# Splitting the expert weights of a fused transformer kernel tile by tile instead of two tiles at a time

## The reference, cut to what matters

```python
x = x + gt1 * (concatenate([na_x, hg_x], axis=-1) @ w_out)      # 4 groups of weights
...
q = (t @ wq)                                                    # 8 groups of weights
s = einsum('tpcd,pckd->tpck', q, sub_keys)                      # scores, then top-16 twice
...
idx, g = ..., softmax(top)
a = gelu(einsum('tpkd,td->tpk', u[idx], t))                     # 64 groups: the up stage
return einsum('tpk,tpkd->td', (g * a), v[idx])                  # the down stage
```

## Time and profile before

| | before |
|---|---|
| median of 3 runs | 2461.55 us |
| the profiled execution | 2461.23 us |
| its span, first to last instruction | 2459.4 us |
| PE busy | 2268.9 us (92%) |
| DVE busy | 1780.3 us (72%) |
| ACT busy | 924.7 us (38%) |
| POOL busy | 629.1 us (26%) |
| groups 0 to 75 on PE | 541 to 1360 us |
| mean granted TensorE clock | 0.973 |

### The profile page before, as it was taken

One profiled execution on the slowest core, in us unless ns is written; L12 is line 12 of the kernel. 1 busy time (PEld: TensorE's weight loads), 2 busy tenths in 40 slices (PEclk: granted clock), 3 DMA queues, 4 the chain that ended last, 5 costly groups with the idle time before them and its releaser, 6 DMA issues. The chain is left out here.

```text
span 2459.4 us, 32296 instructions
## 1 busy us (share of the span) xinstructions
PE 2268.9 (92%) x12787; PEld 2018.9 (82%) x12787; DVE 1780.3 (72%) x2981; ACT 924.7 (38%) x1210; POOL 629.1 (26%) x357
## 2 busy tenths in 40 slices
PE   7999887978998999899999899999999897899997
PEld 2888676756888999899999799999999575677775
DVE  6545687764589999999996687878776657654543
ACT  4222233333232333455563233333333434566332
POOL 0000232311346776532234333333330000000000
PEclk9999998989999999999999999999999999999999
DMA  6567400011236777789889999999995222012221
GB/s 249 199 238 243 148 10 1 1 65 55 87 116 225 240 237 250 249 314 349 323 323 384 354 355 349 356 361 350 348 359 178 87 86 83 29 52 69 68 87 68
DMA packets 178102, 488.72 MB, mean 199 GB/s; under 512 B 13696, under 2 KB 80384, under 8 KB 166432
## 3 DMA queue, kind: packets, MB, share of 16 engines
q1 hardware_dynamic: 141088, 352.43, 41.6%
q0 software_dynamic: 36864, 134.23, 14.2%
HBM read 432.08 MB, written 52.43 MB: 197 GB/s over the span
## 5 line engine op out<-in xcount | busy, mean ns | idle before, releaser
L1054 PE MATMUL ps<-h_high,u_high 128*128 128x384 f32 (+1 forms) x1216 | 430.2, 354 | 43.4 <-POOL u_low L1244 20.8
L1055 PE MATMUL ps<-h_low,u_high 128*128 128x384 f32 (+1 forms) x1216 | 420.7, 346 | 0.0
L1056 PE MATMUL ps<-h_high,u_low 128*128 128x384 f32 (+1 forms) x1216 | 420.7, 346 | 0.0
L1054 PE MATMUL ps<-w_high,v_high 128*128 128x384 f32 x1024 | 343.8, 336 | 12.0 <-DVE w_low L1624 12.0
L1055 PE MATMUL ps<-w_low,v_high 128*128 128x384 f32 x1024 | 343.0, 335 | 0.0
L1056 PE MATMUL ps<-w_high,v_low 128*128 128x384 f32 x1024 | 342.9, 335 | 0.0
L1054 PEld LDWEIGHTS ps<-h_high,u_high 128*128 128x128 f32 x1216 | 230.6, 190 | 58.5 <-POOL u_low L1244 23.6
L1381 ACT ACTIVATE v_high<-v_raw 128x2048 fp32r<-128x2048 f32 x64 | 122.6, 1916 | 347.0 <-PE ps L1056 347.0
L1054 PE MATMUL ps<-h_high,w_high 128*128 128x512 f32 x560 | 227.4, 406 | 24.9 <-DVE h_low L2273 10.3
L1055 PEld LDWEIGHTS ps<-h_low,u_high 128*128 128x128 f32 x1216 | 231.0, 190 | 8.3 <-issue 1.2
L1056 PEld LDWEIGHTS ps<-h_high,u_low 128*128 128x128 f32 x1216 | 230.5, 190 | 8.1
(11 more groups left out here) (424 smaller groups left out, 4464.2 us busy)
## 6 DMA issues: line engine op xcount, KB each, us to landing
v_raw<-in_peer_v SPq DMA_DIRECT2D x64, 1024.0 KB
w_raw<-in_w SPq DMA_DIRECT2D x99, 512.0 KB, 3.6
u_first<-in_uT SPq DMA_DIRECT2D x32, 1024.0 KB
u_second<-in_uT SPq DMA_DIRECT2D x32, 1024.0 KB
xT<-in_late_w SPq DMA_DIRECT2D x56, 512.0 KB, 4.3
gelu_up<-gelu SPq DMA_DIRECT2D x128, 192.0 KB
gates<-gates_sb SPq DMA_DIRECT2D x12, 2048.0 KB
weighted<-gelu_up SPq DMA_DIRECT2D x64, 384.0 KB
```

The lines of the kernel that those rows point to most:

```text
L1054: pe.matmul(out, wh, mh, start=start, stop=False)
L1055: pe.matmul(out, wh, ml, start=False, stop=False)
L1056: return pe.matmul(out, wl, mh, start=False, stop=stop)
```

## The change

The high and the low part of a group are now made by two instructions each, one for each tile, with an access pattern of 8 blocks of 128 values (`tile_of`). The semaphores `u_hi` and `u_split` count tiles instead of groups. ACT may make the high part of tile j of group g+2 when PE has finished tile j of group g, and it does so right behind the evacuation of that tile. PE waits for the low part of each tile. SP still loads whole groups, and still waits for both low parts of the group before.

```diff
+        def tile_of(group, j):
+            return group.rearrange("p (t j c) -> p t j c", j=GE, c=P)[:, :, j, :]
...
                 if g >= 2:
-                    sp.wait_ge(u_split, PIECES_BEFORE + g - 1)
+                    sp.wait_ge(u_split, PIECES_BEFORE + GE * (g - 1))
...
             for x in range(WQ_G + U_G):
                 if x + OUT_G < SPREAD_AT:
-                    pool.wait_ge(u_hi, OUT_PIECES + x + 1)
...
-                    pool.tensor_tensor(u_low[:, x % 2], u_raw[x % 2][:], u_high[:, x % 2].bitcast(F32),
-                                       ALU.subtract).then_inc(u_split, 1)
+                    for j in range(GE):
+                        pool.wait_ge(u_hi, PIECES_BEFORE + GE * (x + OUT_G) + j + 1)
+                        pool.tensor_tensor(tile_of(u_low[:, x % 2], j), tile_of(u_raw[x % 2][:], j),
+                                           tile_of(u_high[:, x % 2], j).bitcast(F32), ALU.subtract).then_inc(u_split, 1)
...
-                pe.wait_ge(u_split, OUT_PIECES + s + 1)
                 for j in range(GE):
                     x = GE * g + j
                     for m in batches_at(g, j):
                         spread(m)
+                    pe.wait_ge(u_split, PIECES_BEFORE + x + 1)
                     bank_free(x)
...
-            def high(x):
-                g = x + OUT_G
-                act.wait_ge(u_in[g % 2], 16 * (g // 2 + 1))
+            def high(g, j):
+                if j == 0:
+                    act.wait_ge(u_in[g % 2], 16 * (g // 2 + 1))
                 if g >= 2:
-                    act.wait_ge(u_mm, GE * (g - 1))
-                act.activation(u_high[:, x % 2], u_raw[x % 2][:], ACT.Copy).then_inc(u_hi, 1)
+                    act.wait_ge(u_mm, GE * (g - 2) + j + 1)
+                act.activation(tile_of(u_high[:, g % 2], j), tile_of(u_raw[g % 2][:], j), ACT.Copy).then_inc(u_hi, 1)
...
                         act.activation(gel[:, x % 4, :], ps[:, x % 4, 0:DENSE], ACT.Gelu).then_inc(u_ev, 1)
-                if g + 2 < GROUPS:
-                    high(g + 2 - OUT_G)
+                    if g + 2 < GROUPS:
+                        high(g + 2, j)
...
-            def low_u(x):
-                dve.wait_ge(u_hi, OUT_PIECES + x + 1)
-                dve.wait_ge(u_split, OUT_PIECES + x)
-                dve.tensor_tensor(u_low[:, x % 2], u_raw[x % 2][:], u_high[:, x % 2].bitcast(F32), ALU.subtract)\
-                   .then_inc(u_split, 1)
+            def low_u(g):
+                for j in range(GE):
+                    x = PIECES_BEFORE + GE * g + j
+                    dve.wait_ge(u_hi, x + 1)
+                    dve.wait_ge(u_split, x)
+                    dve.tensor_tensor(tile_of(u_low[:, g % 2], j), tile_of(u_raw[g % 2][:], j),
+                                      tile_of(u_high[:, g % 2], j).bitcast(F32), ALU.subtract).then_inc(u_split, 1)
```

More of the change, by code:

```diff
@@ L1206, in _ @@
             load(0)
-            sp.wait_ge(u_split, OUT_PIECES + WQ_G + U_G - 1)
+            sp.wait_ge(u_split, PIECES_BEFORE + GE * (GROUPS - 1))
             gate_pair(0)
@@ L1212, in _ @@
             spill(GROUPS - 2)
-            sp.wait_ge(u_split, OUT_PIECES + WQ_G + U_G)
+            sp.wait_ge(u_split, PIECES_BEFORE + GE * GROUPS)
             gate_pair(1)
@@ L1240, in _ @@
                 if x + OUT_G < SPREAD_AT:
-                    pool.wait_ge(u_hi, OUT_PIECES + x + 1)
                     if x == 0:
-                        pool.wait_ge(u_split, OUT_PIECES)
-                    pool.tensor_tensor(u_low[:, x % 2], u_raw[x % 2][:], u_high[:, x % 2].bitcast(F32),
-                                       ALU.subtract).then_inc(u_split, 1)
+                        pool.wait_ge(u_split, PIECES_BEFORE + GE * OUT_G)
+                    for j in range(GE):
+                        pool.wait_ge(u_hi, PIECES_BEFORE + GE * (x + OUT_G) + j + 1)
+                        pool.tensor_tensor(tile_of(u_low[:, x % 2], j), tile_of(u_raw[x % 2][:], j),
+                                           tile_of(u_high[:, x % 2], j).bitcast(F32), ALU.subtract).then_inc(u_split, 1)
                 for n in picks_at[x + OUT_G]:
@@ L1291, in _ @@
             for g in range(OUT_G):
-                pe.wait_ge(u_split, PIECES_BEFORE + g + 1)
                 for j in range(GE):
                     x = GE * g + j
+                    pe.wait_ge(u_split, PIECES_BEFORE + x + 1)
                     bank_free(x)
@@ L1385, in high_w @@
                 act.activation(w_high[:, g % 2], w[:, g % 2], ACT.Copy).then_inc(w_hi, 1)
-            high(-OUT_G)
+            for j in range(GE):
+                high(0, j)
             for t in range(KT):
                 act.activation(h_high[:, t, :], k.mixT[:, t, :], ACT.Copy).then_inc(h_hi, 1)
-            high(1 - OUT_G)
+            for j in range(GE):
+                high(1, j)
             for t in range(KT):
@@ L1394, in _ @@
                 if t in (1, 3, 5):
-                    high((t + 3) // 2 - OUT_G)
+                    for j in range(GE):
+                        high((t + 3) // 2, j)
             act.wait_ge(e_eps, NORMS_BEFORE + 1)
@@ L1400, in _ @@
                 act.activation(h_high[:, t, :], full[:, t, :], ACT.Identity, bias=k.mod[:, 24 + t:25 + t]).then_inc(h_hi, 1)
-            high(1)
+            for j in range(GE):
+                high(OUT_G + 1, j)
             for g in range(OUT_G, GROUPS):
@@ L1468, in low_out @@
             def low_out(g):
-                dve.wait_ge(u_hi, PIECES_BEFORE + g + 1)
-                dve.tensor_tensor(u_low[:, g % 2], u_raw[g % 2][:], u_high[:, g % 2].bitcast(F32), ALU.subtract)\
-                   .then_inc(u_split, 1)
+                for j in range(GE):
+                    dve.wait_ge(u_hi, PIECES_BEFORE + GE * g + j + 1)
+                    dve.tensor_tensor(tile_of(u_low[:, g % 2], j), tile_of(u_raw[g % 2][:], j),
+                                      tile_of(u_high[:, g % 2], j).bitcast(F32), ALU.subtract).then_inc(u_split, 1)
             low_out(0)
@@ L1627, in _ @@
                 if g >= SPREAD_AT:
-                    low_u(g - OUT_G)
+                    low_u(g)
                 for n in dots_at[g]:
```

## The result

| kernel | time, us | ratio to before |
|---|---|---|
| before | 2462.68 median (2455.9 to 2465.86, 20 runs) | |
| after | 2466.11 median (2463.04 to 2470.35, 20 runs) | 1.0015, 95% interval 1.0009 to 1.0021 |

The account below looks back on a forecast made before the run. From 705 to 1000 us DVE, held by POOL's subtracts, ends the chain that PE waits on. -11.5 -0.9 +1 = -11.4 us on 2461.2 gives 2449.8, so 2450; range 2436 to 2468 (forecast's own 2443 to 2458, chance 0.45).

Parts of the forecast that it names:

- the term that decides: DVE, 705 to 1000 us: twelve long waits on POOL fall to one half each; -11.5 us, bounds 0 and -27.
- the second rival: 705 to 1000 us: POOL's halves follow so closely that DVE waits for both; 2459 to 2461 us, chance 0.20.
- signs of being wrong: Wrong if a POOL half needs 3 us, DVE's long waits stay at 4.4 us, or PE waits for a bank.
- PE's side: 705 to 1000 us: PE's waits for POOL's `u_low`, 20.8 us before, could shrink by 15 us, to under 8.
- PE's wait for `peer_sel`: At group 43's transposes, near 1000 us: grows from 0.7 to between 2 and 10 us.
- The start: DVE's first subtract, group 0: starts about 0.85 us sooner, and PE with it, carried through; -0.9 us.
- The spread stretch: Groups 44 to 75, DVE making low parts: 0.1 us more per group to group 67; net +1 us, 0 to +3.
- The sizes: Half-size instructions: POOL 2.35 us against 4.6 whole, ACT 1.05 against 1.91, DVE 1.225 against 2.29.
- ACT's wait for loads ahead of the second `gelu`: ACT's new order puts the load wait first; priced zero, up to 5 us if a load landed 5 us later.
- The gain moves into `selected`: Same claim as the second rival: PE waits less for `u_low`, more at the transposes for `selected`; 2459 to 2461, chance 0.20.
- DVE gets slower: 705 to 1000 us: POOL starts more often amid DVE's dots and products; +12 us, 2463 to 2475 us, chance 0.13.
- DVE also sheds half: 705 to 1000 us: DVE waits 24 to 27 us less, PE regains 21.5; 2440, down to 2436 us, chance 0.22.

Follow-up runs that it names:

- the run with POOL and DVE alone: Small kernel without the computation: POOL's pair of half subtracts and one DVE instruction, here with a gather issued ahead; a cast takes up to 5.06 us.
- the two runs with the gap in some groups only: The change, POOL's second half waiting for its first in groups 17 to 43 alone (2456.96 us, 0.9970) or 4 to 16 alone (2466.13 us, 1.0010).
- the gap: The change, with POOL's second half waiting for the semaphore of its own first half; 2455.98 us, ratio 0.9966 to before.
- quarters: The change with POOL's subtract in four quarters of 512 values for a group, each waiting for the one ahead; 2463.11 us, ratio 1.0000.
- The run with 64 columns: The change with POOL subtracting only 64 of the 128 columns of each block in groups 4 to 43; 2434.47 us, ratio 0.9879.
- the run with 8 columns: The change with POOL subtracting only 8 of the 128 columns of each block in groups 4 to 43; 2428.88 us, ratio 0.9854.
- the gap with whole parts on DVE: The gap with halves in groups 4 to 43 alone, ACT and DVE instructions whole in the others; 2457.44 us, ratio 0.9974.

## Why the prediction was wrong, point by point

**The step that failed** is in the term that decides: "If no wait can be longer than one half, 2.35 us, they fall to 12 x 2.35 = 28.2 us: 16.5 us gained." Waits of 5.2 us occurred (casts of 5.4), longer than any before (4.5), since a gather's issue of 0.96 us joins POOL's pair and DVE does not get in until all three are over (the run with POOL and DVE alone). The groups 17 to 43, where gathers stand ahead of the pairs, are where it counts (the two runs with the gap in some groups only). The term was to be -11.5 us, with 0 as its upper bound; it is +4.1. Of this difference of 15.6 us the gap, which lets DVE in behind the first half, gives back 9.3 (60.4 to 51.1 us of waits); the other 6.3 us belong to the second error below. The bound was wrong too, though its condition, "if POOL's two halves run back to back without letting DVE in and act like one", came close: I had the mechanism of the second rival, and not what sets it off.

The trace of before does not show the hold: its longest casts and tensor_scalars, 4.0 us, are shorter than one subtract of 4.6 us. What it shows is a gather issued ahead of POOL's subtract, and at 801.82 and 934.35 us a cast that comes during such an issue and loses only 0.2 us. I looked at how long a POOL instruction is, and not at what stands in front of it; and it has no row with two low parts back to back, so a cap of one half was an inference, not a reading. One of the signs of being wrong that it named came in: DVE's long waits did not fall below 4.4 us.

**Under it lies a second error.** Even where the halves do let DVE in, the sum of its waits falls little: 51 us with the gap, 49 with quarters, 56 whole. The next instruction waits instead, since DVE has casts and products in a row. With half of POOL's work the sum is half. That total POOL time decides is what the prediction named and weighed lower. The two runs with fewer columns and the quarters bear it out in the main, with piece length as a correction (0.39 us of waiting for each microsecond of POOL with whole subtracts, 0.29 with pieces of 1.3 us). The prediction drew it from the Trainium skill, "Advanced Engine Details and Errata", section "GPSIMD Details", which states the conflict and gives no price. How long one wait lasts stands in the Trainium skill, "SBUF — State Buffer", section "SBUF: two separate sides": the shared pair is an exclusive lock that goes to one side for a whole instruction. The trace agrees (the cast alone with the pair ends with the first half, at 26.91 us), except behind a gather, where the measured hold spans three instructions, 5.6 us.

The prediction's own price of these waits, some 48 us, left out the eight dots into `row_sum` (4.4 us) and a gate product at 723 us (4.1 us); with them it is the 56.3 us of the table.

**PE's side** was to fall under 8 us of waits and is at 20.1. This goes with DVE: POOL waited 64.2 us for dots instead of 50.3. The early half is there; it is of little use as long as POOL starts late.

**PE's wait for `peer_sel`** was to grow to between 2 and 10 us and is 1.5; `selected` was to come near 987 us and starts at 1000.5. Both belong to the failed term.

**The start**, -0.9 us: measured -0.8. **The spread stretch**, +1 us, from 0 to +3: measured +0.5. Its cost side holds as worked out: from group 44 to group 66 DVE's period is 11.91 us instead of 11.81 (262.0 and 259.8 us for 22 groups). **The sizes** on POOL, ACT and DVE hold within 3%. **ACT's wait for loads ahead of the second `gelu`** does not appear under that name. ACT's idle time ahead of `gelu` that the profile puts down to the stores of `gelu` grew from 139 to 191 us; which part of it is the load that now stands ahead is not shown. PE waited for no bank, so the price of zero holds.

**The rivals.** "The gain moves into `selected`" gave 2459 to 2461 us. Of its two halves one is right, PE and POOL gain nothing; but the waiting did not move to the transposes (L1327 now, 1.5 us), it stayed at `u_low`. "DVE gets slower" gave 2463 to 2475, and the time fell in there, by another mechanism: not the dots, whose waits fell from 17.5 to 14.4 us, but the casts, from 9.1 to 26.5. "DVE also sheds half" was priced at 21.5 us of returned waits. The run with 64 columns, in which DVE's waits are halved, is some 30 us faster than before (POOL also delivers sooner in it), since the clock comes back as well. Against the run with 8 columns a wait of PE in this stretch costs 1.3 to 1.5 times its length (27.6 us for the 21.5 of before, 31.7 for the 21.6 of after), a factor that the sum lacked; here it would have made the error larger.

Why whole subtracts cost 56.3 us and halves 60.4, and not the other way round, hangs on which DVE instructions are caught: now casts, by a gather and both halves, before tensor_scalars and dots, by one whole subtract. Two of the three casts that lose 5.2 us now have a counterpart in before that came 0.55 us into its gather's issue, not 0.37 to 0.39, and lost 0.2. Three kernels with back-to-back halves repeat the 60.4 us to 0.2, but I have no rule that would give the sign ahead, and that stays open. Why the gap with whole parts on DVE (0.9974) loses 7 us behind the transposes, with a longest wait for the one-hots of 7.3 us in place of 4.3, is only partly clear; that PE comes sooner than DVE has made them is argued, not shown.

## What to carry to other kernels

Cutting an instruction on POOL into pieces did not relieve the DVE that shares an interface with it; the waits went mostly by POOL's total time, and more instructions of DVE took their turn at waiting. If you cut, see what POOL issues just ahead (here a gather could join both pieces that followed it back to back), and let each piece wait for the one before: with that gap the kernel is 0.34% faster than before, where the cut alone made it 0.15% slower. Price a wait of TensorE with the slow matmuls behind it.

## What was not expected of the hardware

- An indirect gather's issue on POOL, 0.96 us, and the two subtracts that follow back to back can keep DVE out to the end of the second: a cast of 0.2 us takes up to 5.06 us and a dot of 1.22 us up to 6.09. A dot that comes 1.9 us into the pair still waits to its end (3.81 us). In the two forms in which POOL has nothing to run for a moment (the gap, the wait for the landing), the hold is gone. By the traces of the whole kernels it also does not come about for casts that ask up to 0.24 us, or 0.54 to 0.56 us, into the issue.
- If DVE is in the middle of a dot when the gather is issued (the gather then takes 1.93 us), there is no such hold.
- A wait of POOL on its own semaphore costs 0.1 us: a pair takes 4.76 instead of 4.64 us.
- POOL's subtract of 512 values takes 1.27 us, of 1024 values 2.34 us alone and 2.40 us in the kernel, of 2048 values 4.6 us: nearly in proportion, with an estimated 0.2 us fixed (1.27 and 2.34 us for 512 and 1024 values).
